# Moving three attention rounds, their masks and the decay steps among the projection blocks of a hybrid RWKV-7 and attention step

## The reference, cut to what matters

```
x = x + 1/2 * SwiGLU_1(rmsnorm(x))
h = rmsnorm(x);  P = h @ w_in      (r|k|v|low-rank parts, attention q|k|v, branch gates)
A = RWKV-7 time mixing             (decay, delta-rule state update, group norm)
B = dilated sliding-window attention, 12 heads of 64, 3 head groups
x = x + (sigmoid(gA) * (A @ w_branch_rwkv) + sigmoid(gB) * (B @ w_branch_attn)) @ w_out
x = x + 1/2 * SwiGLU_2(rmsnorm(x))
```

## Time and profile before

| | |
|---|---|
| median of three runs | 2333.81 us |
| profiled execution, its own time | 2333.82 us |
| profiled execution, span from first to last instruction | 2331.9 us |
| PE busy | 2315.6 us, 99% of the span |
| DVE busy | 1458.2 us, 63% |
| ACT busy | 982.2 us, 42% |
| POOL busy | 111.6 us, 5% |
| 16 DMA engines, weight queue | 50.8% |
| mean granted TensorE clock | 0.999 |

### The profile page before, as it was taken

How to read it: one execution, slowest core, us unless ns; L and a number is a source line. 1 busy time by engine, 2 the same in 40 slices (tenths; PEclk the granted TensorE clock), 3 DMA queues, 4 the chain that set the end, 5 groups by cost and what they waited for, 6 DMA issues and landing times.

```text
span 2331.9 us, 57524 instructions
## 1 busy us (share of the span) xinstructions
PE 2315.6 (99%) x23128; PEld 2289.8 (98%) x23128; DVE 1458.2 (63%) x2000; ACT 982.2 (42%) x1257; POOL 111.6 (5%) x194
## 2 busy tenths in 40 slices
PE   9999999999999999999999999999999999999999
PEld 9999999999999999989998999999999999999999
DVE  6555455555556668878776767766555555545554
ACT  6333333333334554565222446544333333333333
POOL 0000000000002123000000000120000000000000
PEclk9999999999999999999999999999999999999999
DMA  6666567555555767435333636655555555555555
GB/s 242 202 225 213 182 213 247 182 181 181 181 176 167 234 201 238 159 128 195 113 102 113 225 123 217 213 189 176 180 183 182 181 181 180 182 182 183 181 164 172
DMA packets 125617, 429.82 MB, mean 184 GB/s; under 512 B 15256, under 2 KB 21528, under 8 KB 124960
## 3 DMA queue, kind: packets, MB, share of 16 engines
q1 hardware_dynamic: 117504, 393.49, 50.8%
q0 software_dynamic: 7968, 34.20, 4.6%
HBM read 415.14 MB, written 21.33 MB: 187 GB/s over the span
## 4 chain that ended last, share of the span: by engine, by line
PE 93%; DVE 4%; ACT 1%; DVEq 1%; issue 1%; DMA 0%; ACTq 0%; SPq 0%
PE bank L266 30%; PE bank L267 29%; PE bank L268 29%; PE bank L1292 3%; DVE wlo L239 2%; ACT whi L233 1%; DVE kkey L1118 0%; DMA x<-in_x 0%; DVE cum L1130 0%; PE bank L1334 0%; DVE mx L1161 0%; ACT rkv L687 0%; PE bank L1645 0%; PE bank L1419 0%; DVEq L1160 0%
## 5 line engine op out<-in xcount | busy, mean ns | idle before, releaser
L239 DVE TENSOR_TENSOR wlo<-raw,whi 128x1024 fp32r<-128x1024 f32 (+3 forms) x794 | 913.4, 1154 | 595.4 <-ACT whi L233 592.2
L266 PE MATMUL bank<-hhi,whi 128*128 128x264 f32 x4048 | 1164.1, 288 | 3.7 <-DVE wlo L239 2.9
L233 ACT ACTIVATE whi<-raw 128x1024 fp32r<-128x1024 f32 (+3 forms) x794 | 792.5, 1001 | 865.0 <-PE bank L268 848.2
L267 PE MATMUL bank<-hlo,whi 128*128 128x264 f32 x4048 | 1148.0, 284 | 0.0
L268 PE MATMUL bank<-hhi,wlo 128*128 128x264 f32 x4048 | 1146.8, 283 | 0.0
L266 PEld LDWEIGHTS bank<-hhi,whi 128*128 128x128 f32 x4048 | 763.1, 189 | 12.7 <-issue 4.3
L267 PEld LDWEIGHTS bank<-hlo,whi 128*128 128x128 f32 x4048 | 763.6, 189 | 1.1
L268 PEld LDWEIGHTS bank<-hhi,wlo 128*128 128x128 f32 x4048 | 759.9, 188 | 0.0
L266 PE MATMUL bank<-mhi,whi 128*128 128x264 f32 x1408 | 399.5, 284 | 0.0
L268 PE MATMUL bank<-mhi,wlo 128*128 128x264 f32 x1408 | 398.9, 283 | 0.0
L267 PE MATMUL bank<-mlo,whi 128*128 128x264 f32 x1408 | 398.9, 283 | 0.0
(11 more groups left out here) (268 smaller groups left out, 1655.6 us busy)
## 6 DMA issues: line engine op xcount, KB each, us to landing
raw<-in_weights SPq DMA_DIRECT2D x666, 512.0 KB, 3.3
raw<-in_weights SPq DMA_DIRECT2D x64, 384.0 KB, 3.1
out_skv<-in_cache POOLq DMA_DIRECT2D x16, 512.0 KB, 3.8
raw<-in_weights SPq DMA_DIRECT2D x32, 256.0 KB, 3.3
raw<-in_weights SPq DMA_DIRECT2D x32, 192.0 KB, 2.5
side<-stg POOLq DMA_DIRECT2D x18, 132.0 KB, 3.6
gates<-side POOLq DMA_DIRECT2D x1, 2376.0 KB, 13.1
x<-in_x SPq DMA_DIRECT2D x4, 528.0 KB, 6.5
```

The lines of the kernel that those rows point to most:

```text
L233: act.activation(whi[:, u % RING, 0:n], raw[:, u % RING, 0:n], ACT.Copy).then_inc(hi_done, 1)
L239: dve.tensor_tensor(wlo[:, s, 0:n], raw[:, s, 0:n], whi[:, s, 0:n].bitcast(F32), ALU.subtract).then_inc(lo_done, 1)
L266: pe.matmul(bank[:, 0:T], hi, xhi[:, k], start=(k == 0), stop=False)
L267: pe.matmul(bank[:, 0:T], hi, xlo[:, k], start=False, stop=False)
```

## The change

The rounds are four blocks apart in place of three. In PE's order a round is now: scores in the middle of block 10+4r, probabilities turned at the end of block 12+4r, values in the middle of block 13+4r. So the values of a round stand ahead of the scores of the next, and the two waits change: the values wait only for the copied probabilities, and the next scores wait for the copied values. DVE masks ahead of its second split (in place of behind it). ACT copies the turned probabilities right behind its first split of iteration 13+4r. The tables of the RWKV preparations are new. The high part of the attention result is made in iteration 22, and the low part in two halves, in iteration 23 and in the second block of the gates.

```diff
-REMOVAL_AT = {3: 0, 4: 1, 6: 2, 7: 3, 8: 4, 9: 5, 15: 6, 20: 7}
-SUMS_AT = {11: 0, 12: 1, 14: 2, 17: 3, 18: 4, 21: 5, 22: 6, 23: 7}
-DECAYED_AT = {12: 0, 14: 1, 17: 2, 18: 3, 21: 4, 22: 5, 23: 6, 24: 7}
+REMOVAL_AT = {3: 0, 4: 1, 6: 2, 7: 3, 8: 4, 9: 5, 20: 6, 21: 7}
+SUMS_AT = {11: 0, 12: 1, 13: 2, 15: 3, 16: 4, 17: 5, 19: 6, 22: 7}
+DECAYED_AT = {12: 0, 13: 1, 15: 2, 16: 3, 17: 4, 19: 5, 22: 6, 24: 7}
...
             for m in range(3 * RT):
                 hi("rkv", m, 0)
+                for rnd in range(ROUNDS):
+                    if m == 13 + 4 * rnd:
+                        probs_act(rnd)
...
-                if 11 <= m <= 17 and m % 3 == 2:
-                    exp_act(m // 3 - 3)
+                if m in (11, 15, 19):
+                    exp_act((m - 11) // 4)
...
-                if 11 <= m <= 17 and m % 3 == 2:
-                    scaled(m // 3 - 3)
+                if m in (11, 15, 19):
+                    scaled((m - 11) // 4)
...
                 for rnd in range(ROUNDS):
-                    if m == 12 + 3 * rnd:
-                        probs_act(rnd)
-                    elif m == 14 + 3 * rnd:
+                    if m == 13 + 4 * rnd:
                         values_act(rnd)
-                if m == 3 * RT - 1:
+                if m == 3 * RT - 2:
                     act.wait_ge(u_vec, 5)
...
+                for rnd in range(ROUNDS):
+                    if m == 10 + 4 * rnd:
+                        masked(rnd)
                 if m < 2:
                     rotated(2 * AT - 3 + m)
...
-                    if m == 11 + 3 * rnd:
+                    if m == 11 + 4 * rnd:
                         n = len(heads_of(rnd))
...
-                for rnd in range(ROUNDS):
-                    if m == 10 + 3 * rnd:
-                        masked(rnd)
                 if m == 3 * RT - 1:
                     dve.wait_ge(ob_high, 1)
-                    dve.tensor_tensor(obl[:], ob, obh[:].bitcast(F32), ALU.subtract).then_inc(ob_done, 1)
+                    ob_low(0)
...
                     to_spill(n - 1)
+                    ob_low(3)
                 lo("gates", n, 1)
+                if n == 1:
+                    dve.drain()
...
+        def ob_low(j):
+            dve.tensor_tensor(obl[:, j:j + 3], ob[:, j:j + 3], obh[:, j:j + 3].bitcast(F32), ALU.subtract).then_inc(ob_done, 1)
...
-                    if m == 10 + 3 * rnd:
+                    if m == 10 + 4 * rnd:
                         scores(rnd)
-                    elif m == 12 + 3 * rnd:
-                        probs(rnd)
-                    elif m == 14 + 3 * rnd:
+                    elif m == 13 + 4 * rnd:
                         values(rnd)
                 block_pe("rkv", m, (2, 3))
+                for rnd in range(ROUNDS):
+                    if m == 12 + 4 * rnd:
+                        probs(rnd)
...
-            pe.wait_ge(ob_done, 1)
+            pe.wait_ge(ob_done, 2)
...
-                pe.wait_ge(prob_out, rnd)
-                if rnd > 1:
-                    pe.wait_ge(value_out, rnd - 1)
+                pe.wait_ge(value_out, rnd)
...
         def values(rnd):
             pe.wait_ge(prob_out, rnd + 1)
-            if rnd < 2:
-                pe.wait_ge(score_out, rnd + 2)
-            else:
-                pe.wait_ge(value_out, rnd)
```

## The result

The changed kernel is slower: 2341.61 us (median of 8 runs, 2336.67 to 2344.45) against 2333.76 (8 runs). The ratio is 1.0028, 95% interval 1.0017 to 1.0039. The profiled execution took 2341.76 us, with a span of 2339.8. In the repeat at the end of the experiments the ratio was 1.0017 (1.0008 to 1.0026), with a median of 2339.12: still slower, and by about 4 us in place of 8.

What follows compares the result with a forecast made beforehand. PE's own work was taken to bound the kernel, with ACT and DVE's split loop a second bound between 984 and 1105 us. 2333.8 - 0.6 (first chunk) = 2333.2, + 3.0 (two clock falls) = 2336.2 us; range 2331.5 to 2339.2.

Steps and rivals of the forecast that it cites:

- The split loop: Alternation of ACT and DVE between 984 and 1105 us, a second bound; 7.5 us per turn with a running sum.
- the two new waits: PE's values in rounds 0 and 1 wait for ACT's copied probabilities: 3.7 and 3.2 us in place of 2.0 and 1.5.
- PE's path without the clock: PE's work and waits up to the first chunk product, put at 1096.9 against 1096.54: 0.4 us later.
- a fall costs 1.5 us: Price of PE's clock falling to 1.2 GHz behind each of the two new waits: + 3.0 us in all.
- the low clock lasts: Rival: low clock behind PE's long waits in blocks 13 and 17 costs two stretches of 1.5 each: 2339.2 us, chance 0.12.
- low clock for more than 7 us in all: Sign that would show the forecast wrong; the forecast expected some 3.4 us of low clock behind each long wait.
- The first chunk, minus 0.6 us: DVE starts the first chunk 0.6 us earlier, so PE goes on at 1102.1 in place of 1102.75.
- the list of signs: Observations that would show the forecast right or wrong, among them a PE wait under 0.5 us in the first chunk.
- Fewer falls: Rival: PE's clock falls behind only one new wait (2334.7 us) or neither (2333.2 us); chance 0.31.
- the same 3.9 us: Masks ahead of DVE's second split were to take 3.9 us as before, same engine, same turn.

Runs made afterwards that it cites:

- e1: The changed kernel with 24 filling matmuls, result thrown away, ahead of the values of rounds 0 and 1: 2337.76 us, ratio 1.0010.
- e13: The changed kernel run again, unaltered, on one chip with the kernel before: 2339.12 us, ratio 1.0017.
- e6: The kernel before with masks ahead, low part in halves and the new tables, rounds still three blocks apart: 2337.89 us, ratio 1.0014.
- e7: The changed kernel with the running sums of iterations 12 and 16 moved to other iterations: 2340.58 us, ratio 1.0032.
- e8: The kernel before with only the low part in halves and the high part in iteration 22: 2336.31 us, ratio 1.0007.
- e10: The changed kernel with tables laid anew, no sum in turns with masks or ahead of ACT's copy: 2333.92 us, ratio 0.9992.
- e5: The kernel before with masks ahead of DVE's second split, low part in halves and high part in iteration 22: 2331.29 us, ratio 0.9984.
- e3: The kernel before with only the masks moved ahead of DVE's second split: 2329.97 us, ratio 0.9977.
- e15: Repeat of e3, unaltered, on the same chip as the other repeats: 2329.00 us, ratio 0.9975.
- e11: e10 with the low part back in one piece and the high part, both in iteration 23; added drain kept: 2331.91 us, ratio 0.9979.
- e4: The kernel before with only the three new tables of the RWKV preparations: 2334.99 us, ratio 1.0002.

## Why the prediction was wrong

The forecast was no measurable change, 2336.2 us, range 2331.5 to 2339.2. Measured: 2341.61, outside and slower; the repeat's 2339.12 lies at the upper end of the range.

- *The split loop and the two new waits* were right. Iteration 13 was put at 1008.9 and starts at 1009.01; the values were to start at 1010.3 and start at 1010.49; the waits were put at 3.7 and 3.2 and are 3.56 and 3.30. No wait for masks, none for low parts, none before the last round's values.
- *PE's path without the clock*: the first chunk product at 1096.9. The runs with filling matmuls have it at 1097.5 and 1097.9. Right within a microsecond.
- *The clock is the step that failed*, "a fall costs 1.5 us". That price came from a fall with PE already running, near the start. In the changed kernel's profile the clock falls while PE still stands in its waits of 3.6 and 3.3 us, and it stays low for about twice as long, for 5.5 us of PE's work. From the values to the scores it takes 10.02 and 10.19 us, where e1 has 7.46 both times: 2.6 and 2.7 us, 5.3 in all in place of 3.0. The chunk product came at 1102.7, not at 1099.9. This is the rival "the low clock lasts", which I had given 0.12, and its sign, low clock for more than 7 us in all, is there. The price was carried over from a wait half as long, and no row of the kernel before had one of the new length. The price is not fixed by the length either: the long waits of e13, e6 and e7 cost 1.4 to 1.7 us where the low clock lasted some 3.4 us.
- *The first chunk, minus 0.6 us, failed too.* The wait did fall from 1.0 to 0.4 us, as the list of signs says, but not because DVE comes earlier. PE comes later: without falls (e1) it goes on behind this wait 116.53 us after the first scores, and 116.49 in the kernel before, so nothing is won. DVE starts its `ak` 115.71 us after the first scores in e1 and 115.66 before. The loop was to be 2.0 us ahead at the first split of block 25 and is 0.8 (1096.79 in e1 against 1097.58), and the second half of the low part takes 0.9 of DVE's time again. Nor do halves win by themselves: in e8 the turn of iteration 23 takes 7.5 us as before, though half of the low part is gone from it. That the remaining wait is near the forecast is luck.
- *The rest of the miss* lies behind the first chunk, 2.4 us later in this profile than in that of before (1.7 if counted from the chunk product). The two profiles of the kernel before differ by 2.5 us in the same part, so this can't be told from variation. By PE's times the three parts are 2.3 (clock), 0.8 (no gain in the chunk, and scores that start 0.2 later) and 2.4: 5.5 us.
- *The rival "Fewer falls"* happens in single runs: 3 of the first 8 and 3 of the 11 of e13 have a mean granted clock of 0.999 in place of 0.996 to 0.998. Of the first 8 two of these are the fastest (2336.67 and 2337.61); even they are above its 2334.7.
- *The tables* were counted as cover for other work, and the turns with sums ahead of the copy were taken as given. The runs show that the long waits, and with them the loss, come from there: the rounds as they are, with other tables, have a ratio of 0.9992 (e10) where the change has 1.0028 and 1.0017, and the tables cost 6.6 us on the three-block rounds with masks ahead too (e6 against e5), by another wait.
- *Masks ahead* were counted as "the same 3.9 us". In the old rounds they are worth 5 to 6 us (e3, e15), because they fill a time in which DVE waits for ACT. In the four-block rounds DVE waits for PE's scores instead. What masks ahead are worth there was not run by itself; with other tables and one low part (e11) the four-block rounds reach a ratio of 0.9979, which can't be told from e3's 0.9977.

On the clock the Trainium skill ("TensorE: Matmul & The Clock Gate", section "HAM oscillation — how this bites in real kernels") says that a long enough stand-still between bursts of matmuls brings the lower level, and that keeping the array busy avoids it. The runs agree: 1.00 with filling matmuls (e1), 0.52 from 1009 to 1016 us without.

On the halves the Trainium skill ("Perfetto Trace Analysis", section "Optimizing Scalar/DVE Operations") says that breaking up instructions may let work be done sooner where DVE or ACT hold up another engine. Here it did not: the second piece landed in DVE's queue ahead of the first chunk's work, and PE's wait there went from 1.0 to 2.1 us (e8, e5).

## What to carry to other kernels

Where three engines are ordered by hand, ask of each moved step what stands ahead of it in its own engine's order: a copy of 1.5 us began 4.9 us after its data were there (1004.0 to 1008.89), because ACT had first to wait for DVE's running sum; without that sum (e10) it began 3.6 us earlier. Put such cross-engine relays (sum, then exponential) into iterations that nobody waits for, and long steps of one engine into the time in which it waits for another anyway: one such move by itself, masks ahead, beat both versions (2329.0 us, ratio 0.9975). Price a wait of TensorE by its length plus the low clock behind it, and give that price as a range: here it was 1.4 to 2.7 us for waits of 2.5 to 3.8 us, and none or 1.5 for about 2 us.

## What the runs showed of the hardware that I had not expected

- Behind PE's long waits the low clock lasted either some 3.4 or some 6.8 us (estimates from one-microsecond stretches), and the longer one does not go with the longer wait. 6.8 us: both waits of the changed kernel (3.56 and 3.30) and the second of e13 (3.31), each with the fall 0.9 to 1.3 us before PE resumed. 3.4 us: e13's first (3.57), both of e6 (3.54 and 2.51), e7's 3.81 and 3.44, and e4's 2.78, each with the fall at most 0.5 us before PE resumed, or after it.
- The cost beyond the wait was 2.6 to 2.7 us for the long form and 1.4 to 1.7 for the short one.
- Waits of 2.1, 2.0 and 1.86 in this part of the kernel cost none. Near the start one of 1.87 us was followed by a fall in the profile of before and by none in e1's.
- From the first chunk product to the end, where the versions differ only in the chunk's wait (2.1 us at most), it takes 1235.0 to 1239.6 us, and with that wait left out the spread is no smaller (1228.8 to 1233.4 from where PE goes on). A difference of 2 us between two single profiles of this kernel is no evidence; the same length read off inside the profile, over the part in question, repeats within 0.1 us where the clock is not involved (104.7, 104.7 and 104.7; 110.3 and 110.4).
